# Attention: the running maxima are turned by three transposes of 4 or 2 columns a head, and laid into the row by transfers of 512 bytes

## The reference

```
z = rms_norm(x) @ w_in
oa = mla_mixer(...)        # group A, 4 heads: q and k of 64 + 32 dimensions
ob = dilated_mixer(...)    # group B, 4 heads: windows, dilation, a bias by distance
oc = gqa_axial_mixer(...)  # group C, 8 query heads on 2 key/value heads
x = x + rms_norm(concat(oa, ob, oc) @ w_out)
x = x + rms_norm(conv_gated_mlp(rms_norm(x)))
```

## Time and profile before

| | us |
|---|---|
| three runs | 3770.8, 3768.0, 3770.8; median 3770.79 |
| the profiled execution | 3768.39 |
| its span | 3766.6 |
| PE busy | 3660.8 (97%) |
| DVE busy | 1843.0 (49%) |
| ACT busy | 1568.9 (42%) |
| POOL busy | 1141.5 (30%) |

### The profile page before, as it was taken

The page is one execution under the profiler, slowest core; times in us unless marked ns, Lnnn a source line. Parts: engine busy times, 40 slices in busy tenths (PEclk is TensorE's granted clock), DMA queues, the critical chain, the costliest instruction groups (busy, mean ns, idle before and its releaser), DMA issues. The chain is left out here.

```text
span 3766.6 us, 49891 instructions
## 1 busy us (share of the span) xinstructions
PE 3660.8 (97%) x18327; PEld 3020.0 (80%) x18327; DVE 1843.0 (49%) x2914; ACT 1568.9 (42%) x2531; POOL 1141.5 (30%) x827
## 2 busy tenths in 40 slices
PE   8999999989999999999989999999899999999998
PEld 7777777768788888888767877777787888888886
DVE  4133878954543333434541357689464333434335
ACT  4334877974312212221342357789642222221213
POOL 1233453433412122121342244434343122121123
PEclk9999999999999999999999999999999999999999
DMA  5412221113111111111323222211231111111113
GB/s 165 126 56 81 72 64 25 39 40 119 55 34 35 44 39 39 33 41 37 112 66 121 70 77 76 55 32 33 68 101 36 43 39 39 33 41 37 33 45 112
DMA packets 203404, 227.43 MB, mean 60 GB/s; under 512 B 14688, under 2 KB 163206, under 8 KB 203207
## 3 DMA queue, kind: packets, MB, share of 16 engines
q1 hardware_dynamic: 203247, 225.37, 20.0%
HBM read 173.86 MB, written 51.48 MB: 60 GB/s over the span
## 5 line engine op out<-in xcount | busy, mean ns | idle before, releaser
L220 PE MATMUL ps<-hh,wh 128*128 128x512 f32 (+1 forms) x2688 | 970.0, 361 | 26.7 <-PEq L214 17.1
L221 PE MATMUL ps<-hl,wh 128*128 128x512 f32 (+1 forms) x2688 | 955.8, 356 | 0.0
L222 PE MATMUL ps<-hh,wl 128*128 128x512 f32 (+1 forms) x2688 | 954.8, 355 | 0.0
L2447 POOL TENSOR_TENSOR wl<-raw,wh 128x1024 fp32r<-128x1024 f32 x126 | 301.7, 2401 | 1267.2 <-ACT wh L2280 1267.2
L220 PEld LDWEIGHTS ps<-hh,wh 128*128 128x128 f32 x2688 | 510.9, 190 | 105.4 <-issue 23.5
L221 PEld LDWEIGHTS ps<-hl,wh 128*128 128x128 f32 x2688 | 511.0, 190 | 76.8 <-issue 5.7
L2508 DVE SCALAR_TENSOR_TENSOR cb<-ps,params,cb 128x1023 f32<-128x1023 f32 (+1 forms) x172 | 143.9, 878 | 870.4 <-ACT cb L2289 870.4
L222 PEld LDWEIGHTS ps<-hh,wl 128*128 128x128 f32 x2688 | 510.0, 190 | 72.5
L1538 DVE TENSOR_TENSOR pl<-ps,ph 128x512 fp32r<-128x512 f32 (+1 forms) x576 | 375.2, 652 | 55.0 <-ACT ps L1383 54.6
L1492 DVE TENSOR_REDUCE mx<-ps 128x1 f32<-128x512 f32 x480 | 330.6, 689 | 141.7 <-PE ps L1297 82.8
L1382 ACT ACTIVATE ph<-ps 128x512 fp32r<-128x512 f32 (+1 forms) x576 | 329.7, 572 | 158.4 <-PE ps L1263 153.3
(11 more groups left out here) (254 smaller groups left out, 5684.2 us busy)
## 6 DMA issues: line engine op xcount, KB each, us to landing
raw<-in_w_up SPq DMA_DIRECT2D x88, 512.0 KB, 3.9
heads<-stage SPq DMA_DIRECT2D x38, 640.0 KB, 3.5
raw<-in_w_down SPq DMA_DIRECT2D x44, 512.0 KB, 3.7
rq<-heads SPq DMA_DIRECT2D x56, 320.0 KB, 4.8
raw<-in_w_in SPq DMA_DIRECT2D x32, 512.0 KB, 5.0
rk<-heads SPq DMA_DIRECT2D x32, 320.0 KB, 4.7
raw<-in_w_out SPq DMA_DIRECT2D x16, 512.0 KB, 4.3
residual<-my SPq DMA_DIRECT2D x32, 256.0 KB, 2.1
```

What stands on the lines that cost most here:

```text
L220: pe.matmul(out, wh, xh, start=(k == 0), stop=False)
L221: pe.matmul(out, wh, xl, start=False, stop=False)
L222: last = pe.matmul(out, wl, xh, start=False, stop=(k == len(pairs) - 1))
L2447: pool.tensor_tensor(c.wl[slot][:], c.raw[parity][:], c.wh[slot][:].bitcast(F32), ALU.subtract).then_inc(w_lo, units)
```

## The change

`turn_row` transposes all four (or two) columns of a row group at once: the stationary side is just these columns, and they come out on four (or two) partitions of 128 columns. ACT copies these partitions into a small tile `row_part` (three of them, one for each r). SP then moves each of its partitions, 512 bytes, by a transfer of its own to its place in the query tile's row, and PE waits for these transfers instead of the copy. Row 2 is turned in step 19 - `max_lead` (6 in group A and for head 8, 7 in B, 5 in the rest of C) instead of step 7. In SP's list the moves of rows 0 and 1 of head h - 2 stand ahead of the q load of head h, that of row 2 between its k or table load and its v load.

```diff
+    c.row_part = [take(f"row_part{i}", [P, P], F32R) for i in range(3)]
...
+    def third_row(h):
+        return 19 - max_lead(h)
...
-        if i == 7 and 0 < h < HEADS:
+        if 0 < h < HEADS and i == third_row(h):
             work.append(("row", h, 2))
...
             @block.sync
+                def move_row(h, r):
+                    t0, t1 = ROW_TILES[r]
+                    sp.wait_ge(row_copied, 3 * h + r + 1)
+                    row = c.q1[h % 3][96:97, :] if kind(h) == "A" else c.q2[h % 3][64:65, :]
+                    for k in range(t1 - t0):
+                        sp.dma_start(row[:, (t0 + k) * P:(t0 + k + 1) * P].bitcast(F32), c.row_part[r][k:k + 1, :].bitcast(F32)).then_inc(row_landed[r], 16)
...
                 for h in range(1, HEADS):
+                    if h >= 3:
+                        for r in range(2):
+                            move_row(h - 2, r)
                     sp.wait_ge(q_hi, 3 * h)
...                  (q load)
                     if not new_kv(h):
+                        if h >= 3:
+                            move_row(h - 2, 2)
                         continue
...                  (k load, table load)
+                    if h >= 3:
+                        move_row(h - 2, 2)
                     sp.wait_ge(v_turned, 2 * n)
...                  (v load)
+                for r in range(3):
+                    move_row(HEADS - 2, r)
                 sp.wait_ge(scored, NS * 14)
...                  (first output weights)
+                for r in range(3):
+                    move_row(HEADS - 1, r)
...
             @block.tensor
-                    if first:
-                        pe.wait_ge(row_copied, 3 * h + block + 1)
+                    if first and h == 0:
+                        pe.wait_ge(row_copied, block + 1)
+                    elif first:
+                        pe.wait_ge(row_landed[block], 16 * row_tiles(block) * h)
...
-                    for k, qt in enumerate(range(*ROW_TILES[r])):
-                        m0 = max_column(qt)
-                        mm = pe.transpose(bank(c, b, P, slice(0, ROW_WINDOW), off=k * P), c.m[:, m0:m0 + ROW_WINDOW], c.ident[:])
-                    mm.then_inc(row_turned, 1)
+                    m0 = max_column(ROW_TILES[r][0])
+                    pe.transpose(bank(c, b, P, slice(0, row_tiles(r))), c.m[:, m0:m0 + row_tiles(r)], c.ident[:]).then_inc(row_turned, 1)
...
             @block.scalar
-                    t0, t1 = (x * P for x in ROW_TILES[r])
-                    row = c.q1[h % 3][96:97, t0:t1] if kind(h) == "A" else c.q2[h % 3][64:65, t0:t1]
-                    act.activation(row, bank(c, b, t1 - t0, slice(0, 1)), ACT.Copy).then_inc(row_copied, 1)
+                    if h >= 2:
+                        act.wait_ge(row_landed[r], 16 * row_tiles(r) * (h - 1))
+                    rows = slice(0, row_tiles(r))
+                    act.activation(c.row_part[r][rows, :], bank(c, b, P, rows), ACT.Copy).then_inc(row_copied, 1)
```

More of the change, by code:

```diff
@@ L1135, in max_lead, with row_tiles @@
         return 13 if h < 4 or h == 8 else 12 if h < 8 else 14
+    def row_tiles(r):
+        return ROW_TILES[r][1] - ROW_TILES[r][0]
+    def third_row(h):
+        return 19 - max_lead(h)
     def side_work(h, i):
@@ L1174, in attention @@
         weights = sem("weights")
+        row_landed = [sem(f"row_landed{i}") for i in range(3)]
         scored, exp_done, p_low, pv_done = sem("scored"), sem("exp_done"), sem("p_low"), sem("pv_done")
@@ L1543, in attention @@
                        v_lo, max_scored, max_taken, max_ready, row_turned, row_copied, scored, exp_done, p_low, m_padded,
-                       pv_done, ln_done, rden_done, scaled, out_hi, out_lo, weights])
+                       pv_done, ln_done, rden_done, scaled, out_hi, out_lo, weights] + row_landed)
 def project_and_normalise(nc, c, L):
```

## The result

The changed kernel takes 3850.6 us in the median (3846.5 to 3856.3, 4 runs) against 3770.8 us: a ratio of 1.021, 95% interval 1.020 to 1.023, some 80 us. The forecast was 3780 us, 9 us more than before, with a range to 3800. The sign was right, the size was not.

The account below looks back on a forecast made before the run. The prediction took PE in the attention phase as the bound. Transposes saved (-23.1 us), waits for transferred rows (+32.5) and DVE (+2) gave +11.4 on the profiled 3768.39 us: forecast 3780 us, range 3758 to 3800.

Parts of the forecast that it names:

- What bounds the kernel: Attention phase: PE is the bound, so PE time removed shortens it one for one and new waits are paid in full.
- The transposes: Row work on PE: 210 of 300 go at 0.11 us each, saving 23.1 us.
- DVE in group C: Weight loads already wait for DVE's maximum at step 7, so between 0 and 4.6 us isn't saved; 2 taken.
- The rooms: Time from a row's copy start to PE's weight load, less transposes between: for row 0, 1.81 to 3.45 us.
- The chain: From the copy's start to the last landing: copy 0.26, SP's wake 0.05, three issues 0.90, landing 1.6; 2.81 us.
- the sum of +11: Whole kernel: -23.1 us of transposes, +32.5 of PE's waits for rows, +2 for DVE, giving +11.4 us.
- The landing: Last SBUF-to-SBUF transfer of a row: 1.6 us taken, near the stores, with 1.2 to 2.4 kept.
- Rival 2: Row transfers land in 2.0 us or more, by fixed price or behind a load: 3794 to 3816 us; chance 0.14.
- The clock: PE's granted clock after waits: the prediction had no term for it.
- rival 1: Copy start to last landing is short enough, balancing at 2.49 us; faster, 3763 us at 2.31; chance 0.21.

Follow-up runs that it names:

- the kernel of transposes alone: Kernel before with one transpose a row group, ACT copying partition 0 repeatedly straight into the row, no transfers, output differs: 3750.2 us, ratio 0.9945.
- the choice of places: Changed kernel with one transfer a row, but row 2 of heads 2 to 7 as before (four transposes, direct copy): 3749.8 us, ratio 0.9949.
- row 2 alone: Changed kernel with rows 0 and 1 as before and only row 2 by transfers: 3825.0 us, ratio 1.0149.
- row 0 earlier: Changed kernel, four transfers a row, row 0 turned at step 14 beside group A, 13 beside C, 15 before B's heads: 3816.6 us, ratio 1.0124.

## Why the prediction was right in sign and wrong in size

- *What bounds the kernel*: right. PE time that goes is given back (20.4 us of a nominal 23.1), a new wait is paid in full, and the traffic beside it is free.
- *The transposes*: right, 0.11 us each. *DVE in group C*: between 0 and 4.6 was the bound, 2 my value; all that is missing from the 23.1 is 2.7.
- *The rooms*: right, within some tenths. In the kernel of transposes alone, row 0's copy starts 2.52, 3.00, 3.46 and 1.8 to 2.0 us ahead of the weight load, for 2.51, 2.99, 3.45 and 1.81 in the text.
- *The chain*: this is the term that failed. "I take 0.30 from issue to issue, 0.90 for three" was 0.6 and 1.8. The transfers I took it from the earlier trace rows fill SBUF from HBM with two small rows; the q loads of the attention phase, in the same queue, had 0.54 us an issue (1.08 for two), and I went by the small ones because of their bytes. I let "the shortest issue in the trace is 0.25 us" stand as a floor and gave the issue no upper end at all, only the landing. With 3.78 in place of 2.81 us, the prediction's own table of rooms gives 39.4 us a layer in place of 16.3, or 3768 + 79 - 21 = 3826. The trace has 38.7 a layer (69.0 + 8.5 us in both). This term is 46 of the 69 us by which the sum of +11 fell short of the measured +80.
- *The landing*: 1.6 taken, 1.7 measured; but behind the k and table loads it rose to as much as 4.0 in head 3, and to about 3 in heads 1 and 2. Rival 2 had named a load ahead as a cause, for heads 3 to 5; the sum had SP come late in head 3, but no longer landing anywhere.
- *The clock*: not in the sum, put at nothing without a word. Behind 13 of the 14 waits of 1.70 us and more the granted clock fell for a while to the lower of its two levels (1.2 GHz); 22 us. The waits I forecast (0.3 to 1.8 us) were nearly all short of that, so the error in the chain opened a second cost.
- *The rivals*: rival 1's balance point, 2.49 us from copy to landing, was borne out: one transfer (0.25 + 0.03 + 1.8 = 2.1 us) is on the fast side of it at 3763, and two pieces (2.6 to 2.7) come out even. That 3763 is also what the text had given for a chain of 2.31 is chance: for 2.1 the same table gives 3758.

## What to carry to other kernels

Where PE is the bound, price a replacement of PE work by a DMA as a chain from the producer's end to the semaphore, with every issue ahead of the last landing counted at the upper end of what issues in that queue take, not at the cheapest one's price; and merge the pieces into one transfer first. Lay that chain beside the room at each place where it is awaited, and use it only where it fits: here merging turned +80 us into -7, and the choice of places -7 into -19. Bound each factor of a product from above as well; a wait of some 2 us on PE may cost nearly twice its length (here 1.95 + 0.16 + 1.7), since the granted clock can fall behind it.

## What the runs showed of the hardware

- An SBUF-to-SBUF transfer took about 0.6 us of SP's queue, whether it held one piece of 512 bytes (median 0.59, mostly 0.50 to 0.70, up to 1.87) or up to four (0.63); its semaphore came 1.7 us after the issue began, in the median.
- A transfer of one 512-byte piece is cut small: the trace counts 9,601 packets more for the 300 transfers, 32 each. One of four pieces adds 8, one of two 4 (600 packets more for 90 transfers), and costs no more to issue. So the cutting isn't what the issue's time goes by; what it goes by stays open.
- The lower clock followed 13 of 14 waits of 1.70 us and more in the changed kernel. In the other kernels it followed some of that length and not others: not the 2.14 and 1.99 us of the one-transfer kernel or the 2.21 and 2.18 of the two-piece one, nor 2.78 us with row 2 alone, nor 3.07 with row 0 earlier. No wait under 1.70 us was followed by it in any of them. What else decides stays open. The matmuls just behind the wait still start at full rate (0.23 us apart, from 544.30 on) and slow down a little later.
